# Seven gather buffers for eight in the first three tiles, and one query weight piece kept resident

## The chip, the cores and the metric

The program runs on one core of one Trainium2 chip. The metric is the device time of one execution in microseconds (us). The kernel before takes 2875.5 us, the median of three runs (2870.83 to 2886.68).

## The reference, cut to what matters

The network is two blocks in float32 on 512 tokens of width 1024. The first block (neighbourhood attention, a convolution branch, a mixture of experts) is not touched by the change. The second block has two kinds of attention, a product with `w_out`, and then a PEER layer. The change lies in the part of the kernel that runs the PEER layer of one tile together with the attention of the next tile. In the reference the PEER layer is:

```
query = (ht @ w_query).reshape(t, PEER_HEADS, 2, PEER_HALF)        # 1024 x (8 heads x 256)
sub_scores = einsum('thpd,hpkd->thpk', query, sub_keys)
half_vals, half_idx = top_k(sub_scores, 16)                        # per half of the key
top_vals, top_pos = top_k(sums of all 16 x 16 pairs, 16)
experts = i1 * 128 + i2;  gates = softmax(top_vals)
def block(xb, eb, gb):                                             # 128 tokens
    u = expert_down[eb]                                            # 128 x 8 x 16 rows of 1024
    act = gelu(einsum('td,thkd->thk', xb, u)) * gb
    vv = expert_up[eb]
    return einsum('thk,thkd->td', act, vv)
```

Each token takes, for each of 8 heads, 16 rows of `expert_down` and 16 rows of `expert_up`. The kernel has the two tables side by side (`expert_pair_2`, rows of 2048 numbers), so that one gather brings both.

## The kernel before, in words

The 512 tokens are 4 tiles of 128. A unit n of the PEER layer is one head of one tile, so there are 32 units, n = 8 times the tile plus the head. A unit has 16 gathers, and gather m = 16 n + r brings, for each of 128 tokens, one row of 8 KB: 1 MB in all (1,048,576 bytes). There are 512 gathers.

**The ring of gather buffers.** `pair` is a list of 11 buffers of 2 x 1024 columns. In the first three tiles (m below `FIRST` = 384) gather m uses buffer m modulo `PAIRS_0`, which is 8; number 7 is the first half of `arena_h`. From m = 384 on all 11 are used, in the order `ORDER`, which begins with those that were not in the small ring. GpSimd (called POOL in the profile) issues the gathers in order at L945. Before each it waits for the semaphore `pair_free` of the gather that had the buffer before (`pair_before`). Before m = 2 it also waits for the last projection (`proj_done`, 18 + PROJS), since `arena_h` and parts of the weight ring hold projection operands until then, and before m = 384 for the attention of the last tile.

**The consumers.** A unit is worked off in 8 parts of two gathers each. VectorE (DVE) forms the dot product of the first half of each buffer with the token's vector (`dot`, L2000) and does in between the top-16 search of unit n + 2. ScalarE (ACT) applies the gelu to two dot products (L1380) and scales two small matrices with them (L1382). TensorE (PE) multiplies the second half of the two buffers with these matrices (`up_sums`, L2687) and its last matmul on a buffer increments `pair_free`. Then POOL can issue the gather of eight later.

**The next tile's attention.** Between the parts, by a plan written out in `planned`, the engines do the steps of the attention of tile t + 1 (`attend`), spread over the first 30 of the 64 parts of tile t. Its tail comes later: norm, turn and product with `w_out` (`attended_b`) at parts 30 to 36, and the eight query products (`query_b`, one per head) at parts 41, 44, 48, 51, 54, 57, 60 and 62. At the turn to the next tile PE repeats the tile's vectors over its partitions (`repeat_rows`, L2700), and these wait for the last query product's result.

**The streamed pieces.** The weights of `w_out` and `w_query` have no place of their own in this phase. For each of the tiles 1, 2 and 3 the SyncE queue (SP) streams 12 pieces of 1 MB (`PIECES` = 4 + H: four of `w_out`, eight of `w_query`, one per head) through two half buffers of `hold_a`, piece i in half i modulo 2 (`piece`, L818). Piece i waits until the piece two before it is used. The same space holds attention operands before, so that the first piece of a tile waits for the tile's last attention step.

Of the kernel before, what the change touches and what calls it, by code (L numbers as in the profile page):

```python
# [27 lines left out]
TT = T // P  # L28
D = 1024
DC = D // P  # L30
CTX = 256
CT = CTX // P
H = 8
# [24 lines left out]
K16 = 16  # L58
PAIRS_0, PAIRS = 8, 11
SCRATCH = 8192  # L60
# [19 lines left out]
def build(nc, A, out):  # L80
    with ExitStack() as ctx:
# [528 lines left out]

        PIECES = 4 + H

        def piece(t, i):

            at = hold_a[:, 2 * D * (i % 2):2 * D * (i % 2) + 2 * D]
            turn = 16 * ((t - 1) * PIECES // 2 + i // 2 + 1)
            there = (slab_in[slot2(S_WQ)], loaded2(S_WQ) + turn) if i % 2 == 0 else (wo_b_in, turn)
            if i < 4:
                return at.rearrange("p (c n) -> p c n", c=4), there, A["w_out_2"][i // 2, i % 2]
            return at.rearrange("p (c n) -> p c n", c=DC), there, A["w_query_2"][i - 4]  # L620

# [76 lines left out]
        def _(sp):  # L698
# [102 lines left out]
            load2(S_WQ + 2)  # L801
            load2(S_WQ + 3)

            sp.wait_ge(q_pe, 2)
# [4 lines left out]
            for t in range(1, TT):  # L809
                sp.wait_ge(o_done, H * TT + (t + 1) * H)  # L810
                for i in range(PIECES):
                    _, (there, _), src = piece(t, i)
                    dst = hold_a[:, 2 * D * (i % 2):2 * D * (i % 2) + 2 * D]
                    if 2 <= i < 6:
                        sp.wait_ge(wo_pe, wo_used(t, i - 2))
                    elif i >= 6:
                        sp.wait_ge(q_pe, wq_used(t, i - 6))
                    sp.dma_start(dst, src).then_inc(there, 16)  # L818
                    if i == 1:

                        sp.wait_ge(attT_pe, 2 * t + 2)
                        load_row(rows_2[1][2], mod2_d[0, 3 * D:4 * D])
                        if t == 1:
                            load_halves(gt2_2, 5 * D)
# [11 lines left out]
        def _(pool):  # L836
# [95 lines left out]
            for n in range(TT * H):  # L932
                pool.wait_ge(ids_done, n + 1)
                for r in range(K16):
# [5 lines left out]
                    if m == FIRST:  # L940
                        pool.wait_ge(o_done, H * TT + UNITS)
                    if pair_before(m) >= 0:
                        pool.wait_ge(pair_free, pair_before(m) + 1)
# [1105 lines left out]
        def _(pe):  # L2049
# [568 lines left out]
            def query_b(t, h):  # L2618
                w, there, _ = piece(t, 4 + h)
                pe.wait_ge(*there)  # L2620
# [6 lines left out]
            def attended_b(t, j):  # L2627
                for half in range(2):
                    w, there, _ = piece(t, 2 * j + half)
                    pe.wait_ge(*there)  # L2630
# [182 lines left out]
```

## Time and profile before

| | |
|---|---|
| median of 3 runs | 2875.5 us |
| profiled execution | 2871.68 us |
| span of its instructions | 2869.9 us |
| PE busy | 2228.0 us, 78% |
| DVE busy | 1504.9 us, 52% |
| ACT busy | 876.0 us, 31% |
| POOL busy | 596.3 us, 21% |
| moved by DMA | 948.46 MB, mean 330 GB/s |
| of these, POOL's queue (gathers) | 556.90 MB |

The profile's page has the busy time of each engine, the span in 40 equal slices of 71.7 us with the DMA engines' busy share and rate, the chain of work that ended last, and groups of instructions by source line. The trace can be asked for the same in any stretch of time. Times in it count from the first instruction. The gathers' phase goes from 1399.5 us, where the first is issued, to the end.

### The profile page before, as it was taken

The page shows a single profiled execution, that of the slowest core. Times are in us where ns is not written, and L with a number is a line of the kernel's source. Part 1 is how long each engine was busy: PE and PEld are TensorE (multiplying, and loading weights), DVE is VectorE, ACT ScalarE, POOL GpSimd, SP SyncE. Part 2 cuts the span into 40 slices and gives each one's busy share as a digit, 9 for nine tenths or more (in the row PEclk, how much of TensorE's full clock was granted, in tenths as well). Part 3 has the DMA queues.
Part 4 walks back from the last instruction along what each step waited for, and adds up shares of the span by engine and source line. Part 5 has one row for each costly group of instructions (what it writes and reads, how often), then busy time and mean ns, then how long its engine had stood idle before and what let it go on. Part 6 is the DMA issues. An engine that isn't in the chain of part 4 may idle for free.

```text
span 2869.9 us, 30058 instructions
## 1 busy us (share of the span) xinstructions
PE 2228.0 (78%) x10252; PEld 1011.8 (35%) x10252; DVE 1504.9 (52%) x3429; ACT 876.0 (31%) x1851; POOL 596.3 (21%) x588
## 2 busy tenths in 40 slices
PE   5997999887777874999977576985779866675554
PEld 2455444432222222755632133531335322321110
DVE  3997844400000003201387666886767777677764
ACT  3105211111001002311365323873238543232221
POOL 1000000100000001000134243342333343344442
PEclk9999999899989997999998788997889888897877
DMA  9785455499999997022589999999998999999996
GB/s 371 276 191 142 180 201 213 150 403 409 411 406 406 405 402 306 28 69 81 196 339 421 414 411 421 367 421 418 416 421 320 389 410 417 420 421 421 421 422 282
DMA packets 155969, 948.46 MB, mean 330 GB/s; under 512 B 18522, under 2 KB 50312, under 8 KB 65982
## 3 DMA queue, kind: packets, MB, share of 16 engines
q0 software_dynamic: 78704, 556.90, 47.4%
q1 hardware_dynamic: 68224, 381.17, 34.6%
q10 hardware_dynamic: 8910, 8.75, 0.9%
q8 instruction: 69, 1.13, 0.2%
q14 instruction: 62, 0.51, 0.0%
HBM read 914.99 MB, written 31.77 MB: 330 GB/s over the span
## 4 chain that ended last, share of the span: by engine, by line
PE 46%; DMA 34%; DVE 10%; ACT 4%; issue 4%; POOL 2%; SPq 0%; DVEq 0%; POOLq 0%; ACTq 0%
PE bank L2053 16%; DMA ring<-in_expert_pair,ids 13%; DMA ring<-in_w_exp_up 12%; PE bank L2687 8%; DMA arena_h<-in_expert_pair,ids 6%; PE bank L2059 6%; PE bank L2343 5%; DVE ring L2000 3%; POOL ring L945 2%; DMA ring<-in_w_mod 1%; DMA ring<-in_w_exp_down 1%; ACT arena_w L1382 1%; DVE arena_h L2000 1%; PE bank L2700 1%; PE bank L2632 1%
## 5 line engine op out<-in xcount | busy, mean ns | idle before, releaser
L2687 PE MATMUL bank<-ring,arena_w 128*32 128x512 f32 x1668 | 566.9, 730 | 353.8 <-ACT arena_w L1382 353.6
L945 POOL DMA_INDIRECT ring<-in_expert_pair,ids x417 | 451.0, 1081 | 1069.4 <-PE bank L2687 682.8
L2053 PE MATMUL bank<-arena_h,ring 128*128 128x128 f32 (+2 forms) x1264 | 362.8, 447 | 4.6 <-ACT arena_h L1186 3.2
L2687 PEld LDWEIGHTS bank<-ring,arena_w 128*32 128x32 f32 x1668 | 100.2, 122 | 676.0 <-ACT arena_w L1382 470.4
L2000 DVE CUSTOM_DVE_ANT_0 ring<-ring,arena_h 128x1024 f32<-128x1024 f32 x232 | 280.2, 1225 | 108.6 <-DMA ring<-in_expert_pair,ids 83.8
L2343 PE MATMUL bank<-ring,arena_h 128*64 128x512 f32 x1056 | 272.8, 676 | 72.6 <-DMA ring<-in_w_exp_up 71.1
L2000 DVE CUSTOM_DVE_ANT_0 ring<-ring 128x1024 f32<-128x1024 f32 x185 | 224.8, 1225 | 78.4 <-DMA ring<-in_expert_pair,ids 72.7
L1717 DVE TENSOR_TENSOR arena_q<-arena_q,bank 128x256 f32<-128x256 f32 x32 | 13.5, 421 | 474.2 <-ACT arena_q L1123 474.2
L1380 ACT ACTIVATE arena_w<-arena_w 128x2 f32<-128x2 f32 x256 | 51.8, 203 | 688.2 <-DVE arena_w L2000 687.5
L2053 PEld LDWEIGHTS bank<-arena_h,ring 128*128 128x128 f32 x1264 | 202.4, 194 | 156.0 <-issue 120.4
L2343 PEld LDWEIGHTS bank<-ring,arena_h 128*64 128x64 f32 x1056 | 89.3, 154 | 253.7 <-issue 203.3
L2687 PE MATMUL bank<-arena_h,arena_w 128*32 128x512 f32 x236 | 155.7, 797 | 15.1 <-ACT arena_w L1382 15.1
L1382 ACT ACTIVATE arena_w<-arena_w 128x32 f32<-128x32 f32 x512 | 136.5, 313 | 8.4
L2356 PE MATMUL bank<-ring,arena_q 128*64 128x512 f32 x528 | 120.6, 597 | 23.0 <-DVE arena_q L1720 22.1
L1430 ACT ACT_TABLE_LOAD x88 | 112.9, 1283 | 1.8
L913 POOL DMA_DIRECT2D ring<-in_w_in x3 | 1.6, 536 | 521.8 <-PE bank L2356 521.8
L1123 ACT ACTIVATE arena_q<-bank 128x256 f32<-128x256 f32 x32 | 12.3, 383 | 311.3 <-PE bank L2343 311.3
L2053 PEld LDWEIGHTS bank<-ring 128*128 128x128 f32 x768 | 94.8, 205 | 29.0 <-issue 29.0
L2053 PE MATMUL bank<-ring 128*128 128x128 f32 x768 | 98.9, 290 | 0.0
L1529 DVE SCALAR_TENSOR_TENSOR arena_x<-arena_x,convc 128x512 f32<-128x512 f32 x120 | 90.2, 752 | 4.3
L2059 PE MATMUL bank<-ring,arena_h 128*128 128x512 f32 x192 | 87.4, 612 | 0.0
L2000 DVE CUSTOM_DVE_ANT_0 arena_h<-arena_h,ring 128x1024 f32<-128x1024 f32 x53 | 64.9, 1224 | 41.7 <-DMA arena_h<-in_expert_pair,ids 41.1
(473 smaller groups left out, 3009.8 us busy)
## 6 DMA issues: line engine op xcount, KB each, us to landing
ring<-in_w_exp_gate SPq DMA_DIRECT2D x33, 2048.0 KB, 19.8
ring<-in_w_exp_up SPq DMA_DIRECT2D x33, 2048.0 KB, 24.1
ring<-in_w_exp_down SPq DMA_DIRECT2D x33, 2048.0 KB, 25.0
ring<-in_w_mod SPq DMA_DIRECT2D x12, 2048.0 KB, 14.5
ring<-in_w_in SPq DMA_DIRECT2D x12, 2048.0 KB, 12.2
ring<-in_w_ada SPq DMA_DIRECT2D x12, 2048.0 KB, 7.8
ring<-in_w_query SPq DMA_DIRECT2D x24, 1024.0 KB, 9.1
ring<-in_w_out SPq DMA_DIRECT2D x12, 1024.0 KB, 9.5
```

The source lines that it names most:

```text
L945: pool.indirect_dma_start(pair[pair_of(m)], None, A["expert_pair_2"], bass.IndirectOffsetOnAxis(ap=ids[n % 2][:, r:r + 1], axis=0)).then_i ...
L1380: link(act.activation(gel[:, k0:k0 + count], dots[:, k0:k0 + count], ACT.Gelu))
L1382: act.activation(sel_q[:, n % 2, k, :], sel_q[:, n % 2, k, :], ACT.Copy, scale=gel[:, k:k + 1]).then_inc(sel_done, 1)
L1430: act.preload_act_table_set(GELU)
L1529: link(dve.scalar_tensor_tensor(out=conv[:, cc, :], in0=u_pad[:, cc, k:k + T], scalar=convc[:, cc, k:k + 1], in1=conv[:, cc, :], op0=ALU.m ...
L2000: dve.tensor_tensor_reduce(buf, buf, h2_q[r % 4], 1.0, 0.0, ALU.mult, ALU.add, dots[:, r:r + 1]).then_inc(dots_done, 1)
L2053: mm = pe.matmul(dst, w[:, c, at], rhs[:, c, :], start=(c == 0), stop=(c == chunks - 1))
L2059: mm = pe.matmul(dst, xT[:, c, t * P:(t + 1) * P], w[:, c, at], start=(c == 0), stop=(c == chunks - 1))
L2343: mm = pe.matmul(bank[2 + b][at, :].rearrange("p (g f) -> p g f", g=2), xbT[b][:, c, :], gu[:, :, c, 256 * half:256 * half + 256], start=( ...
L2356: mm = pe.matmul(bank[6 + b][CAP * j:CAP * j + CAP, :], hidT[b][:, k, CAP * half:CAP * half + CAP], slab(n)[:, half, k, 512 * j:512 * j + ...
L2632: mm = pe.matmul(bank[WO_BANKS[1][j]][:, :], mixT2[1][:, 4 * half + c, :], w[:, c, :], start=(half == 0 and c == 0), stop=(half == 1 and c ...
L2687: mm = pe.matmul(bank[4 + half][at, :], sel_q[:, n % 2, k0 + j, :], pair[pair_of(m + j)][:, D + 512 * half:D + 512 * half + 512], start=Fa ...
```

## The change

`PAIRS_0` goes from 8 to 7. The eighth buffer, the first half of `arena_h` (`kept`), is loaded once with the weights of the last head's query (`w_query_2[7]`), after the last projection. The pieces streamed for each of the tiles 1 to 3 go from 12 to 11. Since 11 is odd, the half buffer and the semaphore's count of a piece now follow its number over all tiles. In the last tile `arena_h` is the first of the 11 buffers again, so that gather 384 waits for the last query product of tile 3.

```diff
-PAIRS_0, PAIRS = 8, 11
+PAIRS_0, PAIRS = 7, 11
...
-        PIECES = 4 + H
+        PIECES, KEPT = 4 + H - 1, H - 1
+        kept = arena_h[:, 0:2 * D]
+
+        def piece_at(t, i):
+
+            g = (t - 1) * PIECES + i
+            turn = 16 * (g // 2 + 1)
+            there = (slab_in[slot2(S_WQ)], loaded2(S_WQ) + turn) if g % 2 == 0 else (wo_b_in, 16 + turn)
+            return hold_a[:, 2 * D * (g % 2):2 * D * (g % 2) + 2 * D], there
 
         def piece(t, i):
...
+            if i == 4 + KEPT:
+                return kept.rearrange("p (c n) -> p c n", c=DC), (wo_b_in, 16)
+            at, there = piece_at(t, i)
+            return at.rearrange("p (c n) -> p c n", c=4 if i < 4 else DC), there
...
             load2(S_WQ + 2)
             load2(S_WQ + 3)
+            sp.wait_ge(proj_done, 18 + PROJS)
+            sp.dma_start(kept, A["w_query_2"][KEPT]).then_inc(wo_b_in, 16)
 
             sp.wait_ge(q_pe, 2)
             sp.wait_ge(o_done, H * TT + H)
...
                     if m == FIRST:
                         pool.wait_ge(o_done, H * TT + UNITS)
+                        pool.wait_ge(q_pe, wq_used(TT - 1, KEPT))
```

## Rows read from the trace of the kernel before

**Rows 1.** The page, DMA in 40 slices: busy tenths, and GB/s moved.

```profile
DMA  9785455499999997022589999999998999999996
GB/s 371 276 191 142 180 201 213 150 403 409 411 406 406 405 402 306 28 69 81 196 339 421 414 411 421 367 421 418 416 421 320 389 410 417 420 421 421 421 422 282
```

**Rows 2.** Windows: start:end, length, busy by engine, granted clock, DMA share, GB/s.

```profile
1430.00:1445.00 15.00, 14.13 (x116) 10.85 (x116) 7.19 (x17) 11.38 (x22) 0.00 (x0) 1.00 0.00 1
...
1460.00:1610.00 150.00, 104.70 (x498) 37.85 (x499) 118.84 (x296) 84.99 (x172) 58.80 (x57) 0.81 1.01 421
1610.00:1660.00 50.00, 33.38 (x145) 10.90 (x143) 34.23 (x80) 13.45 (x33) 17.87 (x17) 0.83 0.98 397
...
1800.00:1810.00 10.00, 10.00 (x50) 5.10 (x50) 8.88 (x24) 9.49 (x16) 2.93 (x3) 1.00 0.59 220
...
1840.00:1860.00 20.00, 20.00 (x118) 11.77 (x118) 15.82 (x42) 15.07 (x26) 8.97 (x8) 1.00 0.90 348
...
2010.00:2020.00 10.00, 8.67 (x66) 3.07 (x62) 9.61 (x20) 4.95 (x13) 5.41 (x5) 0.79 0.97 379
...
2160.00:2170.00 10.00, 9.35 (x47) 4.73 (x47) 9.12 (x21) 9.26 (x17) 2.06 (x2) 1.00 0.61 227
...
2180.00:2190.00 10.00, 9.82 (x51) 5.04 (x50) 9.43 (x22) 9.72 (x17) 5.17 (x5) 1.00 0.91 320
...
2200.00:2230.00 30.00, 30.00 (x204) 18.85 (x202) 19.89 (x49) 19.38 (x31) 11.37 (x10) 1.00 0.77 291
...
2280.00:2310.00 30.00, 28.36 (x166) 13.03 (x164) 21.21 (x54) 21.19 (x41) 12.62 (x12) 0.93 0.85 318
...
2390.00:2400.00 10.00, 8.77 (x80) 4.99 (x77) 7.82 (x21) 4.99 (x13) 7.63 (x6) 1.00 0.98 390
...
2513.00:2835.00 322.00, 186.01 (x864) 44.11 (x865) 232.81 (x545) 86.48 (x249) 139.49 (x129) 0.81 1.01 421
```

**Rows 3.** Gathers (L945) of 1460:1800: who waited for them, and issue to landing.

```profile
  DVE ring L2000: 40.1, 33
...
DMA to landing us min/median/max: 6.6/12.6/18.9
```

**Rows 4.** The same line in 2150:2310, issue to landing.

```profile
DMA to landing us min/median/max: 5.4/9.7/13.9
```

**Rows 5.** Timeline: start us, us, what; a pair's dots, gelu, matmuls, and the reissue.

```profile
1458.03 1.22 DVE L2000 CUSTOM_DVE_ANT_0 ring<-ring,arena_h 128x1024 f32<-128x1024 f32 x1
...
1460.44 0.20 ACT L1380 ACTIVATE arena_w<-arena_w 128x2 f32<-128x2 f32 x1 [1.62 <-DVE arena_w L2000]
...
1461.27 3.61 PE L2687 MATMUL bank<-ring,arena_w 128*32 128x512 f32 x8 [3.48 <-ACT arena_w L1382]
...
1465.67 0.94 POOL L945 DMA_INDIRECT ring<-in_expert_pair,ids  x1 [4.36 <-PE bank L2687]
```

**Rows 6.** POOL's timeline at the start: gathers 2, 7 and 8.

```profile
1402.03 0.94 POOL L945 DMA_INDIRECT ring<-in_expert_pair,ids  x1 [0.30 <-issue]
...
1417.75 0.99 POOL L945 DMA_INDIRECT arena_h<-in_expert_pair,ids  x1 [0.31 <-issue]
1446.11 0.94 POOL L945 DMA_INDIRECT ring<-in_expert_pair,ids  x1 [27.37 <-PE bank L2687]
```

**Rows 7.** SP's timeline: the last two streamed pieces of tile 3.

```profile
2478.22 15.13 SPq L818 DMA_DIRECT2D ring<-in_w_query  x2
```

**Rows 8.** POOL's timeline before the last tile: gathers 383 and 384.

```profile
2512.07 0.94 POOL L945 DMA_INDIRECT arena_h<-in_expert_pair,ids  x1 [0.30 <-issue]
2513.31 1.77 POOL L945 DMA_INDIRECT arena_v<-in_expert_pair,ids  x1 [0.31 <-issue]
```

**Rows 9.** PE's timeline: the last query product of tile 3.

```profile
2519.22 3.84 PE L2053 MATMUL bank<-ring 128*128 128x128 f32 x32
```

**Rows 10.** Streamed pieces (L818), issue to landing, over the whole span.

```profile
DMA to landing us min/median/max: 8.9/9.2/14.3
```

More of the change, by code:

```diff
@@ L608, in proj_bank @@
             return (7, 4, 5)[m - GAP_P - 1] if m > GAP_P else (4, 5, 0)[m % 3]
-        PIECES = 4 + H
-        def piece(t, i):
[L615 to L620, printed above, removed]
+        PIECES, KEPT = 4 + H - 1, H - 1
[5 more added lines that the diff above has]
+            return hold_a[:, 2 * D * (g % 2):2 * D * (g % 2) + 2 * D], there
+        def piece(t, i):
+            if i == 4 + KEPT:
+                return kept.rearrange("p (c n) -> p c n", c=DC), (wo_b_in, 16)
+            at, there = piece_at(t, i)
+            return at.rearrange("p (c n) -> p c n", c=4 if i < 4 else DC), there
         def wo_used(t, q):
@@ L811, in _ @@
                 for i in range(PIECES):
-                    _, (there, _), src = piece(t, i)
-                    dst = hold_a[:, 2 * D * (i % 2):2 * D * (i % 2) + 2 * D]
+                    dst, (there, _) = piece_at(t, i)
+                    src = A["w_out_2"][i // 2, i % 2] if i < 4 else A["w_query_2"][i - 4]
                     if 2 <= i < 6:
@@ L2618, in query_b @@
             def query_b(t, h):
-                w, there, _ = piece(t, 4 + h)
+                w, there = piece(t, 4 + h)
                 pe.wait_ge(*there)
@@ L2628, in attended_b @@
                 for half in range(2):
-                    w, there, _ = piece(t, 2 * j + half)
+                    w, there = piece(t, 2 * j + half)
                     pe.wait_ge(*there)
```

## The prediction

> **What bounds the kernel now.** I read the slices first [rows 1]. Every slice from the 22nd on, bar the last, has the DMA engines at eight tenths or more, and most move 411 to 422 GB/s. I then cut this phase into windows [rows 2]. From 1460 to 1610 us the DMA share is 1.01 at 421 GB/s while PE is busy 104.70 of 150 us and DVE 118.84: the transfers are the limit, no engine is. The same holds from 2513 to 2835 us, in the last tile, where the ring has 11 buffers: 421 GB/s. A gather of 1,048,576 bytes at 421 GB/s takes 2.49 us, and so does a streamed piece.
>
> The reader is then to look for the windows where the share falls below 0.99. Between 1460 and 2513 us there are nine: 1610 to 1660, 1800 to 1810, 1840 to 1860, 2010 to 2020, 2160 to 2170, 2180 to 2190, 2200 to 2230, 2280 to 2310 and 2390 to 2400 [rows 2]. I call them dry spells: a consumer was late, all eight buffers were full or held, and the queue of transfers ran down. In two of them PE has no idle time at all (20.00 of 20, 30.00 of 30). In the three in the middle of a tile (1610, 2010, 2390) PE has slack.
>
> Third, the wait of the consumer. Between 1460 and 1800 us DVE waited for gathers into the ring 33 times, 40.1 us in all [rows 3]. So the consumer follows the DMA there, and whatever delays the DMA delays the end.
>
> **How much depth the ring needs.** The life of a buffer has two parts. The transfer: issue to landing takes 12.6 us in the median where the DMA is full [rows 3], but most of that is queueing, since the shortest is 5.4 us [rows 4]. The use: a pair's first dot product starts at 1458.03, ACT's gelu at 1460.44, PE's eight matmuls at 1461.27, and the buffers' next gathers begin at 1465.67 [rows 5]: 7.6 us. With the shortest transfer that is 13.0 us, and the twin of the pair, which has to land too, adds 2.5: some 15.5 us. The DMA gives a ring of eight 8 x 2.49 = 19.9 us for a round, a ring of seven 17.4 us. The spare falls from 4.4 us to 1.9. The ring of seven can still feed the DMA when all goes evenly, but each hiccup of the consumer longer than about 2 us, rather than 4, now lets the queue run down.
>
> One rule of the Trainium skill bears on this. DMA: Bandwidth & Descriptors, section on the anatomy of one DMA on the gpsimd path, has a fixed part of about 2.0 us and a part of bytes over 436 GB/s for each DMA. By it a lone gather would take 4.4 us, an estimate from that page, against the 5.4 us of [rows 4], which has POOL's 0.94 us inside. The rule alone would have two gathers in flight suffice, so that the eighth buffer would be free to give away and the change would gain 6 us; that is the first rival below. The measured use of 7.6 us is what it leaves out.
>
> **The change part by part.**
> 1. Three pieces gone, one for each of the tiles 1 to 3. The last two pieces of tile 3 are issued from 2478.22 to 2493.35 [rows 7], in a stretch where the DMA is full, and so are those of the other tiles. A piece lands 9.2 us after its issue [rows 10], and for all that time takes rate from the gathers. Value: 3 x 2.49 = 7.5 us gained. Bounds: 0, if a consumer were late at all three; 7.5.
> 2. The resident load. The last projection is done by 1402.03 at the latest, as gather 2, which waits for it, is issued then [rows 6]. So 1 MB is added near 1400, with SP's four row loads behind it. The first gathers share the rate with it, but none of them is used before the first unit starts, and from 1430 to 1445 us the DMA share is 0.00 [rows 2]: 15 us of cover for 2.5 us of load. Cost nothing; without the cover 2.5.
> 3. One gather less ahead at the start. Gather 8 waits 27.37 us for the first matmuls [rows 6]. In that pause eight gathers lay ready; now seven do. The eighth megabyte moves behind the pause: +2.5 us, since the DMA is full from 1460 on. Bounds 0 and 2.5.
> 4. The dry spells. A late consumer stops the ring one gather sooner, so each spell grows by 2.49 us of DMA time. It costs that only if the consumer later catches up with the DMA before the next spell. The spell at 1840 follows that at 1800, and those at 2180 and 2200 follow that at 2160, with PE busy all through: these I count as no further loss. Six remain: 6 x 2.49 = 15 us. Bounds: 0 (by the row of median 9.7 us, twice the shortest, at 2150 to 2310 [rows 4], most gathers there were early enough) and 9 x 2.49 = 22.4.
> 5. New dry spells where there are none before. The shortest landing in the stretch to 1800 us is 6.6 us [rows 3], near the 5.4 of an empty queue: the queue is nearly down at times even where the share reads 1.01. I take one new spell a tile, at 2.49 us: 7.5 us. Bounds: 0; and, if the mean issue-to-landing time did not shrink at all with the depth, a round of 12.6 + 7.6 = 20.2 us over seven buffers, 2.89 us each, which over the 384 gathers less their 2.49 would be 150 us. The value is near the low end as the row of 5.4 shows that latency does shrink.
> 6. The entry to the last tile. Gather 384 is issued at 2513.31 [rows 8]; now it waits for the last query product, 2519.22 + 3.84 = 2523.06 [rows 9], and nothing behind it on POOL can pass. Gather 383 needs the buffer of 376 now, which is free somewhat later than that of 375. So two or three gathers are in flight when the pause ends, and five may follow at once. The first of them needs 5.4 us, those in flight last 5 to 7.5. Value +1.5 us; bounds 0 and 9.7 (the whole delay of 384).
> 7. The last query product no longer waits for a piece, but pieces land well ahead of their use, so there is nothing to win. Renumbered halves and semaphore counts: no instruction added but a few waits. Nothing.
>
> Sum: -7.5 + 2.5 + 15 + 7.5 + 1.5 = +19 us. The profiled execution has 2871.68 us, of which 1.8 lie outside the span, so 2890.7 on its scale. The median of the runs shown is 3.8 us above it: 2894.5, and I predict 2894 us.
>
> **The rivals.**
> - A, depth to spare: the change is faster. Mechanism: the removed 3 MB of the stretch up to 2513 count in full, and the queue holds out over each hiccup, because what it loses in depth it wins back in shorter landings. For it: DMA share 1.01 in the long windows, with a median landing of 12.6 us against a shortest of 5.4. Against it: nine spells in which eight buffers did not suffice. It decides if spells grow by less than 7.5 / 9 = 0.8 us each. Time: 2875.5 - 7.5 + 1.5 = 2869.5 us. Chance 0.15.
> - B, between: the spells at the turns of tiles are bound by PE throughout, and only the start and the two or three spells in the middle of tiles count: -7.5 + 2.5 + 3 x 2.5 + 1.5 = +4, or 2879.5 us. Chance 0.2.
> - C, the ring becomes the bound: with 1.9 us spare most waits of POOL for PE, such as the 4.36 us of [rows 5], run the queue down, and the gathers' rate falls by 5% over the 1050 us to 2513: 52 us, less 7.5. Time 2920 us. Chance 0.2.
> - D, the change doesn't do what it says: the streamed bytes fall, but the freed share is taken by nothing, as the gathers are bound by depth already. Then only the costs stand: +26.5, or 2902 us. Chance 0.05.
> - My forecast: chance 0.4, its own range 2885 to 2907 us.
>
> **How the numbers follow.** A measurement of this kernel tells about 0.5%, 14.4 us, from no change. Faster by more than that needs a gain of twice what step 1 can give: 0.03, taken from rival A. The rest of A, B, and 0.03 of my forecast's lower end lie within it: 0.35. The rest, 0.62, is slower. The range reaches from A's time to somewhat over C's: 2868 to 2925.
>
> **What would show it.** Step 1: POOL's and SP's bytes between 1400 us and the end fall by 2 MB, with 33 streamed pieces. Step 3: seven gathers before the pause near 1430. Steps 4 and 5: the windows at the same places have a lower DMA share, median issue to landing falls by about 2.5 us from 12.6, and the gathers' phase up to number 384 gets longer by about 17 us. Step 6: gather 384 begins just after the last query product, and the DMA share in these 10 us is 0.8 to 1. The last tile itself keeps its length. I am wrong if the DMA share of the first three tiles doesn't fall, or falls by over 4%.

## The result, and the profile after

The changed kernel takes 2908.79 us, the median of four runs (2907.43 to 2911.95), against 2873.16 us before (2866.07 to 2886.68): a ratio of 1.0112, 95% interval 1.0075 to 1.0149. (Ratios, here and below, are formed from all fast runs of both kernels; the quotient of these two medians is 1.0124.) It is slower by 35.6 us. I had forecast 2894 us, slower by 18.5. The measured time is inside the range of 2868 to 2925 us, but the loss is nearly twice the forecast one, and just above the 2885 to 2907 us that I had given to my own mechanism.

The profiled execution has a span of 2908.0 us, 38.1 more than before. From the traces I take three marks: the first gather's issue, the first dot product, and the last matmul on a gathered buffer.

| | first gather issued | first dot product | last matmul (L2687, L2696) | first dot to last matmul |
|---|---|---|---|---|
| before | 1399.5 us | 1435.9 us | 2856.0 us | 1420.1 us |
| changed | 1410.8 us | 1447.1 us | 2893.6 us | 1446.5 us |

So 26.4 us are lost where the change works and 11.3 us before it, in a part of the program that is the same. But the 26.4 hold a difference in one unit that the ring doesn't make. Unit 18 takes 51.5 us before and 44.0 in the changed kernel. Four profiles cut at it, in order before (with ten us inside it), experiment 2 (eight buffers), changed, experiment 4 (the changed kernel again); behind the length stand the busy times of PE, its weight load, DVE, ACT and POOL, then granted clock, DMA share and GB/s:

```profile
2247.00:2299.00 52.00, 48.67 (x196) 18.59 (x194) 36.27 (x89) 33.85 (x62) 17.22 (x16) 0.78 0.93 373
2270.00:2280.00 10.00, 10.00 (x26) 4.42 (x24) 7.00 (x17) 4.92 (x10) 1.87 (x2) 0.50 1.01 420
```

```profile
2250.00:2294.00 44.00, 39.50 (x192) 16.07 (x190) 36.08 (x89) 31.84 (x60) 17.39 (x16) 0.96 1.01 417
```

```profile
2280.00:2324.00 44.00, 39.39 (x190) 16.01 (x192) 35.77 (x89) 32.13 (x59) 17.47 (x16) 0.96 0.99 390
```

```profile
2282.00:2336.00 54.00, 51.16 (x194) 20.14 (x192) 36.19 (x90) 32.27 (x60) 17.38 (x16) 0.75 0.83 328
```

The length of this unit goes with TensorE's granted clock: at a mean of 0.94 to 0.96 it takes 43.8 to 45.1 us in seven profiles, and at 0.74 to 0.85 it takes 47.1 to 55.9 us in the other six. Where the clock is the same, eight and seven buffers are alike (43.9 and 44.0 us above). In the kernel before, PE is at the lower of its two levels (0.50) from 2270 to 2280 us, without a gap, after ten us in which it had been busy for 6.67. Both ring sizes are in both groups, but the clock was high in five of seven profiles with seven buffers and in one of five with eight, so that some influence of the ring on the clock is not excluded. Outside unit 18 the phase from first dot to last matmul is 1368.6 us before and 1369.9 in its repetition, 1402.5 changed and 1406.9 in its repetition. The change therefore costs 34 to 37 us in this phase, not 26.4.

The page of the changed kernel, the same two rows as [rows 1]:

```profile
DMA  9784545599999997022399999999998999999997
GB/s 374 265 201 127 213 166 207 209 401 400 403 400 391 392 396 290 1 87 99 155 384 421 371 417 417 357 412 398 378 419 315 402 395 383 421 394 422 421 422 291
```

Slices that had 410 to 421 GB/s now have dips to 371, 398, 378, 395, 383 and 394. To find them I cut both traces at the same places of the work, by the dot products that open units 1, 4, 5, 8, 12, 13, 20, 21 and the middle of unit 23. First the kernel before, then the changed one (columns as above); the windows are in order units 1 to 3, unit 4, unit 8, unit 12, unit 20, second half of unit 23:

```profile
1474.00:1604.00 130.00, 87.76 (x408) 31.28 (x405) 100.15 (x250) 67.41 (x139) 51.02 (x49) 0.81 1.01 421
1604.00:1655.00 51.00, 35.67 (x142) 11.88 (x144) 36.29 (x87) 15.67 (x38) 15.20 (x15) 0.79 0.98 399
1796.00:1838.00 42.00, 39.26 (x250) 21.30 (x242) 35.60 (x84) 39.66 (x68) 13.90 (x13) 1.00 0.91 366
1967.00:2017.00 50.00, 36.05 (x144) 11.72 (x144) 36.56 (x88) 15.91 (x38) 15.22 (x15) 0.80 1.00 409
2343.00:2392.00 49.00, 34.09 (x140) 11.12 (x136) 35.55 (x86) 14.98 (x37) 16.11 (x15) 0.80 1.01 414
2508.00:2533.00 25.00, 22.66 (x176) 11.41 (x176) 14.99 (x35) 9.94 (x23) 14.42 (x13) 0.98 1.01 420
```

```profile
1488.00:1618.00 130.00, 84.33 (x408) 28.93 (x406) 100.13 (x251) 67.87 (x139) 51.24 (x48) 0.81 1.01 421
1618.00:1673.00 55.00, 36.77 (x144) 12.29 (x142) 36.28 (x87) 15.50 (x38) 15.24 (x15) 0.77 0.89 355
1814.00:1856.00 42.00, 39.26 (x249) 21.52 (x242) 35.75 (x85) 39.77 (x69) 14.73 (x14) 1.00 0.87 351
1989.00:2045.00 56.00, 36.43 (x142) 12.25 (x140) 36.06 (x87) 15.38 (x38) 14.60 (x15) 0.77 0.86 342
2372.00:2427.00 55.00, 36.26 (x142) 12.32 (x140) 35.46 (x86) 14.84 (x36) 14.40 (x15) 0.77 0.86 346
2543.00:2568.00 25.00, 22.67 (x176) 11.42 (x176) 15.11 (x35) 10.02 (x23) 9.62 (x11) 0.97 0.85 339
```

The reader is to see four things. The even stretch, units 1 to 3, is as long as before and as full here: seven buffers can feed the DMA at 421 GB/s. They don't always, as the repetitions show below. The turn, unit 8, is as long as before to the microsecond, with less DMA in it. The units in the middle of a tile, 4, 12 and 20, are 4, 6 and 6 us longer at the same work of every engine, and their rate falls to 342 to 355 GB/s. And the last half unit before the last tile has lost 0.15 of its DMA share.

A measure of it that I use below is the lost DMA time: the length of a stretch less its bytes at 421.5 GB/s. For unit 12, by the rows above, it is 50 x (1 - 409/421.5) = 1.5 us before and 56 x (1 - 342/421.5) = 10.6 us after. From the exact bounds it is, in us:

| unit | 4 | 12 | 20 | 8 | 16 | second half of 23 |
|---|---|---|---|---|---|---|
| before | 2.7 | 1.5 | 0.9 | 5.6 | 9.2 | 0.1 |
| changed | 8.7 | 10.5 | 9.9 | 7.0 | 11.0 | 4.9 |

What happens in unit 12 of the changed kernel stands in POOL's timeline:

```profile
1993.24 1.35 POOL L954 DMA_INDIRECT ring<-in_expert_pair,ids  x1 [7.62 <-PE bank L2696]
1994.89 0.93 POOL L954 DMA_INDIRECT ring<-in_expert_pair,ids  x1 [0.30 <-issue]
...
2003.76 1.31 POOL L954 DMA_INDIRECT ring<-in_expert_pair,ids  x1 [7.94 <-PE bank L2696]
...
2019.05 0.94 POOL L954 DMA_INDIRECT ring<-in_expert_pair,ids  x1 [7.77 <-PE bank L2696]
...
2028.20 0.93 POOL L954 DMA_INDIRECT ring<-in_expert_pair,ids  x1 [6.37 <-PE bank L2696]
...
2041.40 0.94 POOL L954 DMA_INDIRECT ring<-in_expert_pair,ids  x1 [11.02 <-PE bank L2696]
```

and the same place in the kernel before, where the gathers at 1971.06 and 1972.94 us are 198 and 199, as are those at 1994.89 and 2003.76 us above:

```profile
1971.06 1.57 POOL L945 DMA_INDIRECT ring<-in_expert_pair,ids  x1 [8.02 <-PE bank L2687]
1972.94 0.93 POOL L945 DMA_INDIRECT arena_h<-in_expert_pair,ids  x1 [0.30 <-issue]
...
2012.76 0.94 POOL L945 DMA_INDIRECT ring<-in_expert_pair,ids  x1 [11.05 <-PE bank L2687]
```

DVE at dot 199, before, and then in the changed kernel, there with the residual addition:

```profile
1983.55 1.23 DVE L2000 CUSTOM_DVE_ANT_0 arena_h<-arena_h,ring 128x1024 f32<-128x1024 f32 x1 [2.56 <-DMA arena_h<-in_expert_pair,ids]
```

```profile
2012.53 1.23 DVE L2009 CUSTOM_DVE_ANT_0 ring<-ring 128x1024 f32<-128x1024 f32 x1 [8.26 <-DMA ring<-in_expert_pair,ids]
...
2025.66 0.69 DVE L1619 TENSOR_TENSOR ring<-bank,arena_q 128x512 f32<-128x512 f32 x1 [3.37 <-PE bank L2641]
2028.36 0.15 DVE L1624 TENSOR_SCALAR rms_t<-ssq 128x1 f32<-128x1 f32 x1 [1.29 <-ACT ring L1098]
2030.19 0.16 DVE L1452 RECIPROCAL rms<-rms 128x1 f32<-128x1 f32 x1 [1.68 <-ACT rms L1100]
```

PE in the changed kernel, with its two products with `w_out` (L2641):

```profile
1993.38 7.74 PE L2641 MATMUL bank<-ring 128*128 128x512 f32 x16
2001.05 3.63 PE L2696 MATMUL bank<-ring,arena_w 128*32 128x512 f32 x24
2014.62 3.63 PE L2696 MATMUL bank<-ring,arena_w 128*32 128x512 f32 x8 [9.95 <-ACT arena_w L1391]
2018.18 7.37 PE L2641 MATMUL bank<-ring 128*128 128x512 f32 x16
...
2036.97 6.09 PE L2696 MATMUL bank<-ring,arena_w 128*32 128x512 f32 x14 [9.59 <-ACT arena_w L1391]
```

Two stalls follow each other. The first is longer than before. PE has the first product with `w_out` in its queue, 7.74 us, and the matmuls that free the next buffers stand behind it. With eight buffers, gather 199 uses the buffer of 191, which is free, with that of 190, before this product, so 199 is issued right behind 198. With seven it needs the buffer of 192, which is freed behind the product: it is issued at 2003.76 us, after a wait of 7.94, and DVE stands 8.26 us for it instead of 2.56. The eighth dot of units 4 and 20 has the same: 6.61 us for 3.71, and 7.53 for 3.23. From the first to the eighth dot of the three units the changed kernel takes 67.5 us and the kernel before 51.8. These 15.7 us are all but 1.0 of what the three units have grown by, and the lost DMA time in them rises from 1.9 to 10.7 us. In the repetitions of the two kernels (experiments 4 and 8) the figures are 64.4 and 50.7 us.

The second stall is the residual addition and the norm, where DVE waits for PE's second product and through ACT's root. It is as long in both kernels: POOL's last pause is 11.02 us here and 11.05 before, and the three units take 98.9 us behind the eighth dot, and 97.9 before. But seven buffers hold one gather less for it. The lost DMA time from the eighth dot to the end of the unit rises from 3.2 to 18.4 us over the three units, and the unit behind pays: 5, 13 and 21 are together 8.4 us longer.

The gathers land sooner, as less queues: in the median 10.1 us after issue from 1470 to 1813 us, for 12.6 at the same place before [rows 3], which is the fall of 2.5 us that I had named as a sign:

```profile
DMA to landing us min/median/max: 5.4/10.1/16.2
```

At the entry to the last tile POOL waits for the last query product (L2062), as step 6 had it, but longer:

```profile
2550.95 0.94 POOL L954 DMA_INDIRECT ring<-in_expert_pair,ids  x1 [3.43 <-PE bank L2696]
2559.06 0.94 POOL L954 DMA_INDIRECT arena_h<-in_expert_pair,ids  x1 [7.17 <-PE bank L2062]
```

And SP's resident load with the four row loads behind it is issued ahead of the first gather (1410.84 us):

```profile
1408.83 0.34 SPq L810 DMA_DIRECT2D arena_h<-in_w_query  x1
```

Of the other signs, 33 pieces are streamed, the whole moves 946.36 MB for 948.46, and seven gathers come before the first pause. The DMA share of the first three tiles (first dot of unit 0 to first dot of unit 24) falls from 0.978 to 0.956, inside the 4% that I allowed. The stretch from the first gather to gather 384 grows by 34.4 us, twice the 17 that I had named, and the last tile is 2.5 us longer, where I had said it would keep its length.

### The profile page after: what moved, and what is told of

It is laid out like the page before. It is cut to its first block, busy times and chain, and to the rows that moved or that the text cites. A ratio compares the mean times of both kernels' runs of the same rounds, so it can differ in the third digit from the quotient of the medians.

```text
span 2908.0 us, 30057 instructions
## 1 busy us (share of the span) xinstructions
PE 2235.8 (77%) x10252; PEld 1008.6 (35%) x10252; DVE 1506.1 (52%) x3429; ACT 876.6 (30%) x1851; POOL 596.5 (21%) x588
## 2 busy tenths in 40 slices
DMA packets 155681, 946.36 MB, mean 325 GB/s; under 512 B 18490, under 2 KB 50280, under 8 KB 65950
## 4 chain that ended last, share of the span: by engine, by line
PE 47%; DMA 33%; DVE 11%; ACT 5%; issue 3%; SPq 0%; POOL 0%; ACTq 0%; DVEq 0%; POOLq 0%
DMA ring<-in_expert_pair,ids 19%; PE bank L2062 16%; DMA ring<-in_w_exp_up 12%; PE bank L2696 9%; PE bank L2068 6%; PE bank L2352 6%; DVE ring L2009 4%; PE bank L2641 2%; DMA ring<-in_w_mod 1%; ACT arena_w L1391 1%; PE bank L2709 1%; PE bank L2537 1%; PE bank L2365 1%; DVE smx L1575 1%; PE bank L2547 1%
## 5 line engine op out<-in xcount | busy, mean ns | idle before, releaser
L2696 PE MATMUL bank<-ring,arena_w 128*32 128x512 f32 x1856 | 576.1, 748 | 374.2 <-ACT arena_w L1391 373.8
L954 POOL DMA_INDIRECT ring<-in_expert_pair,ids x464 | 500.6, 1079 | 1115.4 <-PE bank L2696 718.4
L2062 PE MATMUL bank<-arena_h,ring 128*128 128x128 f32 (+2 forms) x1264 | 364.1, 448 | 4.6 <-ACT arena_h L1195 3.2
L2009 DVE CUSTOM_DVE_ANT_0 ring<-ring 128x1024 f32<-128x1024 f32 x232 | 281.8, 1225 | 146.8 <-DMA ring<-in_expert_pair,ids 140.7
L2696 PEld LDWEIGHTS bank<-ring,arena_w 128*32 128x32 f32 x1856 | 102.6, 124 | 705.2 <-ACT arena_w L1391 497.0
L2062 PEld LDWEIGHTS bank<-arena_h,ring 128*128 128x128 f32 x1264 | 203.7, 196 | 155.9 <-issue 120.4
L2062 PEld LDWEIGHTS bank<-ring 128*128 128x128 f32 x672 | 81.9, 203 | 26.3 <-issue 26.3
L2696 PE MATMUL bank<-arena_v,arena_w 128*32 128x512 f32 x144 | 62.8, 800 | 32.3 <-ACT arena_w L1391 32.3
L1509 DVE SCALAR_TENSOR_TENSOR arena_w<-ring,cvec,arena_w 128x512 f32<-128x512 f32 x112 | 84.2, 752 | 4.0
L2062 PE MATMUL bank<-ring 128*128 128x128 f32 x672 | 85.4, 288 | 0.0
```

The costliest lines, as they stand in the source:

```text
L954: pool.indirect_dma_start(pair[pair_of(m)], None, A["expert_pair_2"], bass.IndirectOffsetOnAxis(ap=ids[n % 2][:, r:r + 1], axis=0)).then_i ...
L1509: link(dve.scalar_tensor_tensor(out=acc, in0=w[:, c, :], scalar=cvec[:, vec, c:c + 1], in1=acc, op0=ALU.mult, op1=ALU.add), part_done if c ...
L2009: dve.tensor_tensor_reduce(buf, buf, h2_q[r % 4], 1.0, 0.0, ALU.mult, ALU.add, dots[:, r:r + 1]).then_inc(dots_done, 1)
L2062: mm = pe.matmul(dst, w[:, c, at], rhs[:, c, :], start=(c == 0), stop=(c == chunks - 1))
L2696: mm = pe.matmul(bank[4 + half][at, :], sel_q[:, n % 2, k0 + j, :], pair[pair_of(m + j)][:, D + 512 * half:D + 512 * half + 512], start=Fa ...
```

## The experiments

Eleven kernels ran, in three sets; the kernels of a set share their chip and the runs of the kernel before. Ratios are to the kernel before. Experiment 2 leaves out the last head's weights (its query takes those of the head before), and experiments 9 and 10 leave out those of `w_out` (the products take what lies in the half buffers); the order of work stays and bytes go. The last column is the phase without unit 18; it is 1368.6 us in the first profile of the kernel before and 1402.5 in that of the changed one.

| experiment | ring | median us | before, same chip | ratio, 95% interval | first dot to last matmul us | without unit 18 |
|---|---|---|---|---|---|---|
| 1 ring of seven alone | 7 | 2911.62 | 2878.6 | 1.0102 [1.0072, 1.0133] | 1449.6 | 1405.6 |
| 2 eleven pieces alone | 8 | 2870.74 | 2878.6 | 0.9981 [0.9942, 1.002] | 1409.2 | 1365.3 |
| 3 resident buffer last | 7 | 2900.01 | 2878.6 | 1.0086 [1.005, 1.0121] | 1439.4 | 1395.6 |
| 4 changed kernel again | 7 | 2912.36 | 2878.6 | 1.0103 [1.0073, 1.0134] | 1460.5 | 1406.9 |
| 5 norm later | 7 | 2894.76 | 2884.42 | 1.0047 [1.001, 1.0085] | 1439.2 | 1395.3 |
| 6 spread | 7 | 2901.19 | 2884.42 | 1.0075 [1.0039, 1.0112] | 1446.8 | 1395.7 |
| 7 spread | 8 | 2885.94 | 2884.42 | 1.0019 [0.9986, 1.0052] | 1429.6 | 1382.6 |
| 8 kernel before again | 8 | 2878.18 | 2884.42 | 0.9977 [0.9949, 1.0004] | 1425.7 | 1369.9 |
| 9 no w_out pieces | 8 | 2866.2 | 2881.87 | 0.9943 [0.9917, 0.9969] | 1412.5 | 1363.1 |
| 10 no w_out pieces | 7 | 2894.73 | 2881.87 | 1.005 [1.0018, 1.0082] | 1436.6 | 1391.5 |
| 11 ring of six | 6 | 2997.72 | 2881.87 | 1.0429 [1.0384, 1.0474] | 1532.1 | 1487.8 |

Runs of one kernel scatter by up to 1.5% in these sets (experiment 6), so I read places in the traces beside the medians. Part of the scatter goes with TensorE's clock: in experiment 2 the shortest run, 2859.00 us, has a mean granted clock of 0.889 and the longest, 2898.42 us, one of 0.875.

**1. The ring of seven alone.**

```diff
-PAIRS_0, PAIRS = 8, 11
+PAIRS_0, PAIRS = 7, 11
```

> The kernel before with the ring of seven alone: all twelve pieces a tile are streamed, the freed buffer holds nothing. Theory (depth): the ring's size makes the whole loss, and the three pieces that the change saves give back up to 7.5 us. The gathers' phase (26.4 us longer in the changed kernel than before) is then 30 to 34 us longer here, and the entry to the last tile costs nothing, as gather 384 doesn't wait for the last query. Rival (the resident piece): the load at the start and the new wait at the entry make a good part of it; then this kernel is no more than 20 us over the kernel before. Second question: the changed kernel also spent 11 us more before the first gather, where its program is the same. If that is the program, this kernel has it or not as its layout falls; if it is a matter of the run, it is near the kernel before here.

The whole loss is there: 1.0102, as large as the changed kernel's 1.0103 on the same chip. The phase is 29.5 us over the first profile of before, just under what I expected; without unit 18, where the two had a different clock, it is 37.0 over, and somewhat more than I expected. The lost DMA time of units 4, 12 and 20 is 7.3, 9.1 and 9.6 us, and that of the second half of unit 23 is 0.1: no entry wait here. The rival (the resident piece makes a good part) falls.

**2. The eleven pieces alone.**

```diff
         def piece(t, i):
-            if i == 4 + KEPT:
-                return kept..., (wo_b_in, 16)
-            at, there = piece_at(t, i)
+            at, there = piece_at(t, min(i, PIECES - 1))
...
-            sp.dma_start(kept, A["w_query_2"][KEPT]).then_inc(wo_b_in, 16)
```

> The other half alone: eight buffers, eleven pieces a tile streamed, and nothing resident; the last head's query multiplies with the weights of the head before it, so one piece a tile is left out of the computation's data and the order of work is kept. Theory: the DMA is the bound in the stretches where the twelfth pieces were, so the time falls by up to 3 x 2.49 = 7.5 us, at least 4. Rival (the freed share is taken by nothing): 0 to 1 us. A fall of over 10 us would say that the piece also delayed the last query.

By the runs it is 0.19% faster, an interval that holds no change, and the kernel before against itself (experiment 8) comes out at 0.9977. The traces are sharper. Unit 7 takes 48.4 us for 51.0, unit 15 48.2 for 51.0, and unit 23 48.8 for 51.6: 2.6 to 2.8 us each, 8.2 in all, where a piece's transfer is 2.49. The lost DMA time stays at 2.6, 2.1 and 1.4 us in the middle units. So step 1 holds where the pieces were. Over the whole phase without unit 18 the gain is 3.3 us against the first profile of before and 4.6 against its repetition, as other units, 17 above all (46.3 us for 43.8), were longer here.

**3. The resident buffer last.**

```diff
-ORDER = list(range(PAIRS_0, PAIRS)) + [...]
+ORDER = list(range(PAIRS_0 + 1, PAIRS)) + [...] + [PAIRS_0]
...
                     if m == FIRST:
                         pool.wait_ge(o_done, H * TT + UNITS)
+                    if m == FIRST + PAIRS - 1:
                         pool.wait_ge(q_pe, wq_used(TT - 1, KEPT))
```

> The changed kernel, but in the last tile the buffer with the resident weights comes last among the eleven, and the wait for the last query stands before gather 394 and no longer before 384. Theory: 4.8 us of DMA time were lost in the last half unit before the last tile of the changed kernel (0.1 before), and this gets 3 to 5 us of it back; the gathers' phase goes from 26.4 to about 22 us over before. Rival: the DMA is idle there because seven buffers are full at the turn anyway; then 0 to 1 us.

The lost DMA time of unit 23 goes to 0.2 us (changed: 4.9, and 8.3 in its repetition), and unit 24 takes 35.8 us for 37.8 and 37.7. So the expected 3 to 5 us are there. The median is 12 us below the changed kernel's on the same chip, with intervals that overlap; units 23 and 24 together account for 2.0 us of it against the first profile of the changed kernel and 3.7 against the repetition, and the rest is not placed. Its window for the second half of unit 23, to be held against the changed kernel's last row above:

```profile
2535.00:2560.00 25.00, 22.67 (x176) 11.40 (x176) 15.14 (x35) 9.99 (x23) 13.71 (x14) 0.97 1.02 421
```

**4 and 8. Both kernels again.** No edit.

> The changed kernel once more on this chip. The gathers' phase should again be 26 us longer than before, as DMA waits there follow from the order of the work. The 11 us before the first gather (the experts' weights ran at 394 to 400 GB/s and not at 404 to 409) I expect to be a matter of the run and not of the program: then the whole is 27 to 32 us over the kernel before; if it belongs to the program, 36 or more, with the first gather near 1411 us again.

> The kernel before once more, for its profile on this chip. Question: the first gather was issued at 1399.5 us in its first profile, and at 1410.8 and 1410.0 in two of the changed kernel, with other variants between (1401.3, 1404.6, 1405.3). If this is a matter of the run, it can be anywhere from 1398 to 1411 here; if it belongs to the program, 1399.5 again within 2 us. The gathers' phase should be 1418 to 1424 us.

The whole is 33.8 us over the kernel before by medians (1.0103), a little over my 27 to 32. The phase is 1460.5 us, longer than the first time by 14, of which 9.6 are in unit 18 (53.6 for 44.0 us), at a granted clock of 0.75 for 0.96. The kernel before has the same: unit 18 at 51.5 us and 0.78, and at 55.9 us and 0.74 in its repetition, whose phase of 1425.7 us is beyond the 1418 to 1424 that I expected. Without this unit the repetitions lie within 1.3 us of the kernel before and 4.4 of the changed one. One profile's phase is only good to some 10 us if the clock is not looked at.

The first gather was issued at 1410.0 us here and at 1403.7 in the kernel before. Over all 13 profiles it is 1399.5 to 1404.6 in the five with eight buffers, 1401.3 to 1412.9 in the seven with seven, 1404.6 with six, though all run the same work to that point (but for the resident load at its end). The difference lies in the stream of the experts' weights: from 620 to 1020 us it runs at 404 to 409 GB/s in the first profile of the kernel before and at 393 to 403 in that of the changed kernel, and the three profiles with the latest first gather (1410.0, 1410.8, 1412.9) are the three in which 350 MB have been moved last (1157.4 to 1158.8 us, for 1148.8 before). Why this stream is slower in some executions stays open. The 1410.0 here is near the 1411 that I had named for an effect of the program. But experiment 1, which has seven, is at 1401.3, so a ring of seven doesn't force it. Whether the rest is chance stays open too; I count it as no effect of the change, but the medians hold it, and it can be some microseconds of the 35.6.

**5 and 6. The norm later, and the tail spread (on experiment 3's kernel).**

```diff
-LATER = {ST_NORM: 30, ST_TURN: 31, ST_OUT: 32, ST_OUT + 1: 36, ST_COLS: 39}
+LATER = {ST_NORM: 30, ST_TURN: 31, ST_OUT: 32, ST_OUT + 1: 36, ST_ADD: 38, ST_COLS: 40}   # 5
+LATER = {ST_NORM: 30, ST_TURN: 32, ST_OUT: 34, ST_OUT + 1: 37, ST_ADD: 39, ST_COLS: 40}   # 6
...
-                elif s == ST_OUT + 1:        # VectorE and ScalarE
+                elif s == ST_ADD:
                     second_norm(...)
```

> The kernel of the entry experiment (ring of seven, resident weights' buffer last in the last tile) with one step taken apart: the residual addition and norm on VectorE and ScalarE (second_norm) no longer stand in the same part as TensorE's last product with w_out, part 36, but two parts later, and the step that turns the columns at 40 instead of 39. Theory (two consumer stalls close together in the middle of a tile, each of which empties a ring of seven): VectorE stands for 15 us there, waiting for TensorE's product and then for ScalarE; with the product done beforehand the stall is 6 to 8 us, and of the 8 to 9 us of DMA time lost in each of the units 4, 12 and 20 some 3 to 5 come back: 8 to 14 us in all. Rival (the streamed pieces crowd out the gathers there): the pieces come in the same order, so the time stays within 3 us.

> The same with all steps of the attention's tail spread: turn at part 32 and not 31, the products with w_out at 34 and 37 and not 32 and 36, the norm at 39, the columns at 40. Theory: both stalls shrink, and the units 4, 12 and 20 lose 2 to 4 us of DMA time each instead of 8 to 9: 12 to 18 us less than the entry experiment, within 8 us of the kernel before. Rival (crowding by pieces): within 3 us. Also possible: the queries, which keep their parts, now come too soon after the columns, and a new stall appears at parts 41 to 44.

A miss. The lost DMA time of units 4, 12 and 20 falls from 7.8, 8.4 and 7.9 us in experiment 3 to 3.1, 3.2 and 4.6 in experiment 5, as expected, but that of the units behind them, 5, 13 and 21, rises from 0.2, 0.1 and 0 to 3.5, 3.6 and 4.9: the second stall has moved there with the norm. The first stall, which the edit of experiment 5 doesn't touch, is as it was: first to eighth dot take 65.5 us in the three units, for 63.7 in experiment 3. The rows are of unit 12:

```profile
1986.00:2040.00 54.00, 30.66 (x134) 10.01 (x132) 36.17 (x87) 16.72 (x39) 17.68 (x16) 0.75 0.97 397
```

The phase is 1439.2 us for 1439.4, and the 8 to 14 us that I expected back are not in it. The ratio of 1.0047 is below the 1.0086 of experiment 3, with overlapping intervals. Experiment 6 is no better (1.0075; units 4 and 5 together lose 8.0 us in both). But it puts the first product two parts later, so that the buffer which the gather of the eighth dot needs is free before it, and with this the first stall goes in two of three units: DVE waits 0.14 and 0.11 us at the eighth dot of units 12 and 20, and first to eighth dot take 16.9 and 16.7 us, as in the kernel before (unit 4: 2.49 and 21.4). So that stall hangs on where the product stands in PE's queue (the turn, which moved with it by one part, was not tried by itself). The time comes back behind it: the three units take 56.6, 57.0 and 57.1 us in all. By the number, within 3 us, the rival would be right here, but it says little, since the loss moved with the steps and the pieces did not; experiments 9 and 10 decide that.

**7. The spread with eight buffers.** The same edit as in 6, on the kernel before.

> The kernel before, ring of eight and twelve pieces, with the same spread of the steps. It lost only 2.8, 1.5 and 0.8 us of DMA time in the units 4, 12 and 20, so at most 5 us are to be had: 0 to 5 us faster. If it gains 10 or more, the tail of the attention costs something besides dry transfers. This is also the version that may beat both kernels.

Not faster: 1.0019. Units 4 and 5, 12 and 13, 20 and 21 lose 6.0, 6.2 and 5.6 us, where the kernel before lost 2.8, 1.6 and 1.0, and the phase without unit 18 is 14.0 us longer. That the tighter sequence of norm, columns and first queries costs more than the spread brings is my reading, and not tested by itself. No version of mine beats the kernel before; experiment 2 might, but leaves out data that would have to lie somewhere.

**9 and 10. Without the w_out pieces, eight and seven buffers.**

```diff
             def attended_b(t, j):
                 for half in range(2):
-                    w, there, _ = piece(t, 2 * j + half)
-                    pe.wait_ge(*there)
+                    w, _, _ = piece(t, 2 * j + half)
...
-                for i in range(PIECES):
+                for i in range(4, PIECES):
```

> The kernel before, ring of eight, without the four streamed w_out pieces a tile: the products with w_out stay, but multiply with what lies in the two half buffers (wrong numbers, 12 MB less to stream), and wait for no piece. Both theories: 12 x 2.49 = 30 us less at most, probably 20 to 30, since the DMA is the bound around them. It is the reference for the next kernel.

> The same with a ring of seven and nothing else changed. Theory (late consumers empty the smaller ring): the stalls of VectorE and TensorE in the middle of a tile come from the chain of the norm, not from pieces, so the units 4, 12 and 20 still lose 5 to 9 us more DMA time each than with eight buffers, and the whole is 25 to 35 us slower than with eight. Rival (pieces crowd out gathers and delay the product that VectorE waits for): without the pieces the two rings differ by 2 us or less in each of these units, and by under 15 us in all.

Unit 12 with eight buffers, then with seven:

```profile
1976.00:2022.00 46.00, 31.90 (x140) 11.07 (x136) 35.60 (x86) 15.06 (x38) 15.72 (x15) 0.85 0.92 372
```

```profile
1991.00:2042.00 51.00, 34.09 (x142) 11.58 (x140) 35.36 (x86) 14.85 (x37) 15.77 (x15) 0.80 0.82 325
```

In units 4, 12 and 20 the ring of seven loses 12.7, 11.7 and 12.6 us, the ring of eight 4.8, 5.4 and 5.8. The difference, 7.9, 6.3 and 6.8, is what it is with the pieces (6.0, 9.1 and 9.0). First to eighth dot take 59.7 us in the three units with seven and 42.8 with eight, so the first stall is there without the pieces too. So no crowding by pieces is needed, and the rival falls. The medians are 28.5 us apart, and the phases without units 0 and 18 36.6 (unit 0 for a reason told below). A miss stands beside it: 12 MB less brought 15.7 us and not 20 to 30. Where a piece is gone the DMA falls idle in part instead: units 4, 12 and 20 lose 16.0 us for 5.1 with the pieces, since these stretches are not bound by bytes alone. The profile of experiment 9 has a misfortune of its own: from 1434 to 1464 us TensorE's granted clock is 0.50 (1.00 at the same place in experiment 8), with 29.14 of 30 us busy, and unit 0 takes 48.0 us for 38.2.

**11. A ring of six.**

```diff
-PAIRS_0, PAIRS = 7, 11
+PAIRS_0, PAIRS = 6, 11
```

> The changed kernel with one buffer less again, a ring of six (the sixth's place is not used in the first three tiles). By the cycle of a buffer (13.0 us of shortest transfer and use, 15.5 with the twin's transfer) six buffers give 6 x 2.49 = 14.9 us for a round: the ring itself becomes the bound, not only at stalls. Theory: the loss is steep, 60 to 120 us over the changed kernel, and the DMA share falls in the even stretches too (units 1 to 3, 10, 11), where seven buffers still gave 1.00. Rival (each buffer costs a gather per dry spell, linear): about 30 us more, as from eight to seven, and the even stretches stay full.

It is 115.9 us over the kernel before, and 80 to 94 over the changed one (by the medians' distances to the kernel before, and by 1.0429 against 1.0112 and 1.0103), inside the 60 to 120 that I expected. Units 1 to 3 had a rate of 421 GB/s in the changed kernel's first profile, and with six:

```profile
1487.00:1631.00 144.00, 91.62 (x404) 30.23 (x400) 100.19 (x250) 67.45 (x139) 53.60 (x48) 0.76 0.96 376
1631.00:1689.00 58.00, 37.93 (x148) 12.11 (x148) 36.38 (x87) 16.89 (x41) 16.64 (x16) 0.76 0.84 337
1837.00:1886.00 49.00, 44.19 (x250) 23.85 (x242) 36.22 (x85) 40.67 (x70) 15.96 (x14) 0.90 0.79 305
```

These are units 1 to 3, 4 and 8. Now the even stretch is 14 us longer and no longer full, and even the turn, which seven buffers left alone, grows by 7 us. The cost of a buffer is steep, not linear. But the step is not as sharp as this pair makes it: the lost DMA time of units 1 to 3 is 0.2 to 2.0 us in the five profiles with eight buffers and 0.3 to 6.9 in the seven with seven (0.3 and 3.2 in the two of the changed kernel; the rate is 399 GB/s in the worst, experiment 10), and 15.6 with six.

## Why the prediction was right, and where it was not

The sign, the mechanism and most places were as forecast: a ring that falls below what the consumers' pauses need, against three saved pieces. The size was not: +19 us by the sum, 34 to 37 in the phase outside unit 18. That 2908.79 us still lies in the range is owed to the range, which reached over rival C. The sizes by step, from the first pair of profiles and the experiments:

- **Step 1, the pieces: right.** Forecast 7.5 us gained; experiment 2 shows 8.2 in the three units concerned, and the changed kernel 7.0 in the same ones.
- **Step 2, the resident load: right.** It is issued ahead of the first gather, and the first dot product follows the first gather by 36.3 us in both kernels.
- **Step 3, the start: right.** Unit 0 takes 40.4 us for 38.2: 2.2 for a forecast of 2.5.
- **Step 4, the dry spells: the turns right, one unit later.** I had priced six spells of 2.5 us, two of them at the turns, one at 2280 and three in the middle of tiles. (PE is without idle time in three of the nine windows, not two: that at 1800 has 10.00 of 10 us.) Units 8 and 16 take 42.2 and 47.0 us in both kernels, as PE and ACT set their length (39.26 and 39.77 of 42.00 us busy in unit 8). The missing gather is paid in the unit behind: unit 9 takes 43.2 us for 40.4, unit 17 46.7 for 43.8, a transfer each, though unit 17 also took 46.3 with eight buffers in experiment 2. The spell at 2280 was no spell of the program: it went with TensorE's clock in unit 18 of that execution. At a granted clock of 0.96 eight buffers lose 0.5 us of DMA time there (experiment 2), at 0.78 and 0.74 they lose 5.9 and 10.0; seven at 0.96 lose 2.3 to 3.3.
- **Step 5, new dry spells: the term that was mis-sized.** With step 4 it gave the middle of a tile 5 us, 15 in all. Units 4 and 5 together grew by 6.9 us, 12 and 13 by 10.1, 20 and 21 by 8.3: 25.2 in all. The lost DMA time of units 4, 12 and 20 rose by 6.0, 9.1 and 9.0, 24.0 in all. I had reckoned each pause by itself, at one transfer of 2.49 us for one gather less of stock. But there are two pauses in each of these units, a few parts apart. At the first, the missing buffer doesn't cost a transfer: it puts a gather behind PE's product, and DVE waits 2.9, 5.7 and 4.3 us longer for it in units 4, 12 and 20. At the second, which is no longer than before, the smaller stock runs out, and the unit behind pays. That the loss is a matter of the ring's size at these stalls is shown (1, 10), and that the first of them hangs on the product by experiment 6. How the loss divides between the two is read from the rows of three units.
- **Step 6, the entry: mis-sized.** 1.5 us forecast; 4.9 us of DMA time lost in unit 23 and unit 24 longer by 1.8 us measured, and 8.3 and 1.7 in the repetition. I had the pause about right (7.17 us, between gathers 383 and 384) but took the queue before it as full; POOL had waited 3.43 us just ahead of it, for the ring of seven. Experiment 3 shows the cost by its removal.
- **The rest, 11 us before the first gather,** is in no step, and the 13 profiles scatter there by 13 us. In the first pair of profiles it happens to be offset for the most part by the 7.5 us of unit 18.

Of the rivals, A (depth to spare) and D (freed share taken by nothing) fall by experiments 1 and 2. B was right that the turns themselves don't grow, but left out that the unit behind pays, and had the middles too cheap. C, a ring that itself is the bound with even stretches no longer full, is what six buffers give; seven come near it in some executions (experiments 3, 5 and 10 lose 4.2 to 6.9 us in units 1 to 3). That the ring of seven can suffice in even work was right by the cycle of a buffer, 15.5 us against 17.4; for six the same sum gives 14.9, under 15.5, and the even stretch broke down. The two parts of the change nearly cancel outside the ring: experiment 1 without them and experiment 4 with them have the same median (2911.62 and 2912.36 us), and by the lost DMA time of unit 23, 0.2 and 8.3 us, the pieces' 8 us went to the entry wait.

The rule of fixed and variable parts (the Trainium skill, DMA: Bandwidth & Descriptors, the anatomy of one DMA on the gpsimd path) gives about 4.4 us for a lone gather, an estimate from that page; the shortest in the changed kernel is 5.4 us, POOL's issue of 0.94 included, so they agree. What decided here was the use of 7.6 us after the landing and the pauses of 6 to 11 us, which no rule of a single transfer holds.

## What to carry to other kernels

A ring of buffers in front of a saturated DMA is to be sized by the longest pause of its consumers, not by the mean cycle: add transfer without queueing, use, and the pause, and compare with the number of buffers times the transfer of one. By the figures of this case that is 5.4 + 7.6 + 11.0 = 24.0 us, ten buffers; nothing above eight was run in these tiles, so the rule itself is not shown here, only that one buffer less than eight costs. Look for several pauses close together, for there a buffer is worth more than its one transfer. Ask at each pause which transfer the smaller ring puts behind it, and who will stand waiting for that one. Don't expect the loss in the unit of the stall alone, for it can be paid in the next one. And before two profiles are compared by their length, compare the granted clock place by place, for one stretch at the lower level can hide or feign a loss of 7 to 12 us. When a buffer is given to something with a late last use, let it join the larger ring last.

## What the runs showed that I had not expected

The first loss of depth cost 1%, the second over 3%: with eight, seven and six buffers units 1 to 3 moved 415 to 421, 399 to 421 and 376 GB/s. And taking 12 MB of streamed weights away with eight buffers gave back only 15.7 us of the 30 that they take at 421 GB/s. And the one unit that spoiled the first comparison, unit 18, was long or short with TensorE's clock: 55.9 us at 0.74 and 43.9 at 0.96, both with eight buffers.
